# Squares of a head split into rounded parts by halves, and the parts of a head's end at other steps

## The reference

```
proj = h @ w_in;  q, f, i, g = split(proj, 4)
log_f = logaddexp(log(lb), log1p(-lb) + log_sigmoid(f));  k = (1 - lb) * sigmoid(-f)
q = silu(q) * 128 ** -0.5
S_t = diag(f_t) S_{t-1} + k_t v_t^T ;  o_t = S_t^T q_t          # by chunks, per head
o = o * rsqrt(mean(o * o, axis=-1) + 1e-6)                      # per token and head
o = o * out_norm * silu(g);  return o @ w_out
```

## Time and profile before

| | |
|---|---|
| median of 3 runs | 2599.49 us (2598.84 to 2599.61) |
| the profiled execution | 2597.69 us |
| its span, first to last instruction | 2595.9 us |
| TensorE (PE) busy | 2567.7 us, 99% |
| VectorE (DVE) busy | 1739.3 us, 67% |
| ScalarE (ACT) busy | 1172.8 us, 45% |
| GpSimd (POOL) busy | 206.0 us, 8% |
| mean granted TensorE clock | 0.999 |

### The profile page before, as it was taken

How to read it: one execution, slowest core, us unless ns; L and a number is a source line. 1 busy time by engine, 2 the same in 40 slices (tenths; PEclk the granted TensorE clock), 3 DMA queues, 4 the chain that set the end, 5 groups by cost and what they waited for, 6 DMA issues and landing times.

```text
span 2595.9 us, 41811 instructions
## 1 busy us (share of the span) xinstructions
PE 2567.7 (99%) x16880; PEld 2148.2 (83%) x16880; DVE 1739.3 (67%) x2471; ACT 1172.8 (45%) x1844; POOL 206.0 (8%) x245
## 2 busy tenths in 40 slices
PE   8999999999999999999999999999999999999999
PEld 7887878787888887887989878977887888888887
DVE  6454454559999978898725564566667777768573
ACT  6454444536444443356432343244545555554331
POOL 2121222300100001132000000000000000000000
PEclk9999999999999999999999999999999999999999
DMA  4101111235777799983423212121543444487763
GB/s 142 42 26 42 35 41 34 73 124 176 253 242 252 266 375 335 336 294 138 159 87 131 67 60 69 42 76 59 197 157 117 154 154 141 158 326 279 242 223 136
DMA packets 290769, 406.14 MB, mean 156 GB/s; under 512 B 15760, under 2 KB 162704, under 8 KB 290576
## 3 DMA queue, kind: packets, MB, share of 16 engines
q1 hardware_dynamic: 276464, 352.07, 39.7%
q0 software_dynamic: 14112, 51.39, 5.8%
HBM read 314.27 MB, written 89.13 MB: 155 GB/s over the span
## 4 chain that ended last, share of the span: by engine, by line
PE 70%; DVE 6%; DMA 3%; issue 2%; ACT 1%; SPq 0%; DVEq 0%; ACTq 0%
PE ps L973 14%; PE ps L903 7%; PE ps L905 7%; PE ps L901 7%; PE ps L579 3%; PE ps L563 3%; PE ps L566 3%; PE ps L689 3%; PE ps L1160 3%; PE ps L693 3%; PE ps L691 3%; PE ps L1161 2%; PE ps L1165 2%; PE ps L1135 1%; DVE mraw L2460 1%
## 5 line engine op out<-in xcount | busy, mean ns | idle before, releaser
L901 PE MATMUL ps<-Bh,Ah 128*128 128x512 f32 x896 | 349.6, 390 | 1.4 <-ACT vb L1715 1.4
L903 PE MATMUL ps<-Bh,Al 128*128 128x512 f32 x896 | 348.8, 389 | 1.5 <-DVE Al L2336 1.5
L2127 DVE TENSOR_TENSOR Wlo<-Wraw,Whi 128x1024 fp32r<-128x1024 f32 x100 | 124.6, 1262 | 217.5 <-ACT Whi L1533 217.4
L905 PE MATMUL ps<-Bl,Ah 128*128 128x512 f32 x640 | 249.0, 389 | 0.0
L1737 ACT ACTIVATE ftr_h<-ftr_r 128x1024 fp32r<-128x1024 f32 x112 | 118.6, 1059 | 237.6 <-DMA ftr_r<-b_scratch 237.4
L973 PE MATMUL ps<-ftr_l,wgt_h 128*128 128x512 f32 x848 | 210.1, 390 | 4.0 <-DVE ftr_l L2404 4.0
L689 PE MATMUL ps<-Whi,Hh 128*128 128x256 f32 x736 | 212.2, 288 | 0.0
L973 PE MATMUL ps<-ftr_h,wgt_h 128*128 128x512 f32 x848 | 210.0, 390 | 0.0
L973 PE MATMUL ps<-ftr_h,wgt_l 128*128 128x512 f32 x848 | 209.6, 389 | 0.0
L693 PE MATMUL ps<-Whi,Hl 128*128 128x256 f32 x736 | 208.2, 283 | 0.0
L691 PE MATMUL ps<-Wlo,Hh 128*128 128x256 f32 x736 | 208.2, 283 | 0.0
(11 more groups left out here) (383 smaller groups left out, 5463.6 us busy)
## 6 DMA issues: line engine op xcount, KB each, us to landing
b_scratch<-qb SPq DMA_DIRECT2D x224, 256.0 KB, 3.0
wgt_r<-in_m_w SPq DMA_DIRECT2D x112, 512.0 KB, 4.8
ftr_r<-b_scratch SPq DMA_DIRECT2D x112, 512.0 KB, 6.1
pair<-in_m_w SPq DMA_DIRECT2D x128, 256.0 KB, 3.2
mraw<-in_w_ada POOLq DMA_DIRECT2D x64, 512.0 KB, 4.6
Wraw<-in_w_in SPq DMA_DIRECT2D x56, 512.0 KB, 4.1
other<-in_m_w SPq DMA_DIRECT2D x32, 512.0 KB, 5.6
mraw<-in_m_w1T POOLq DMA_DIRECT2D x32, 512.0 KB, 5.1
```

The source lines that it names most:

```text
L901: e.matmul(o, h[:, k, :], Bh[x][:, k, :], start=first and k == 0, stop=False, skip_group_check=not first)
L903: e.matmul(o, l[:, k, :], Bh[x][:, k, :], start=False, stop=False, skip_group_check=not first)
L905: i = e.matmul(o, h[:, k, :], Bl[x][:, k, :], start=False, stop=k == 3, skip_group_check=not first)
L2127: e.tensor_tensor(Wlo[n % 4][:], Wraw[n % 2][:], Whi[n % 4][:].bitcast(F), ALU.subtract).then_inc(*S("w_lo", "v").tick(n))
```

## The change

The squares of a head's outputs are no longer one float32 tile `t1`. ACT squares each half (512 tokens), copies it rounded into `sq_h` (at the place of `t2`), and DVE subtracts that from the square into `sq_l` (at the place of `t1`). Part 3 then sums `sq_h` and `sq_l` of each half with a rounded matrix of ones, `onesR`, in four matmuls of 512 columns. The copy of the outputs to `R1` moves behind the squares on ACT. `onesR` is made once, ahead of the first norm's root. The entries of `tail_steps` become part 0, part 1, nothing, part 2, nothing, nothing, part 3, nothing for heads 0 to 6; head 7 keeps its order.

```diff
--- before.py
+++ after.py
@@ -155,6 +155,8 @@
         near = at("near", [P, 8, 32], F, spare)
         acc, kST, St = sa("acc", 10), sa("kST", 11), sa("St", 12)
         t1, t2, t3 = sa("t1", 13), sa("t2", 14), sa("t3", 15)
+
+        sq_l, sq_h, onesR = sa("sq_l", 13, R), sa("sq_h", 14, R), at("onesR", [P, P], R, spare + 1024)


         H_ = lambda i: HA + 4096 * i
@@ -286,7 +288,8 @@
             return iter([("idle", h, 0)] + [("level", h, l) for l in range(8)])

         def tail_steps(h):
-            return [(("tail", h, i // 2) if i % 2 == 0 else ("idle", h, 0)) for i in range(8)]
+            order = (0, 1, None, 2, None, None, 3, None) if h < 7 else (0, None, 1, None, 2, None, 3, None)
+            return [("idle", h, 0) if p is None else ("tail", h, p) for p in order]

         MIX = [("f_end", 0, None)]
         tail = []
@@ -788,9 +791,11 @@
                             pe.wait_ge(S("q_mul").at((h, 7)), S("q_copy").at((h, 7)), out_at(("tail", h, 1)))
                             i = e.matmul(ps[:, c, :], c3(St)[:, c, :], c3(Qb[h % 2])[:, c, :], start=False, stop=True)
                 else:
-                    pe.wait_ge(out_at(("tail", h, 2), 1))
                     for p, c in enumerate(HALF):
-                        e.matmul(psum[b][:, c], ones[:], t1[:, c], start=True, stop=True).then_inc(
+                        pe.wait_ge(S("const_hi").at(0), S("o_rstd").at((h, p - 2)))
+                        e.matmul(psum[b][:, c], onesR[:], sq_h[:, c], start=True, stop=False)
+                        pe.wait_ge(S("o_gate").at((h, p - 2)))
+                        e.matmul(psum[b][:, c], onesR[:], sq_l[:, c], start=False, stop=True).then_inc(
                             *S("ps_full", b).tick((occ, p)))
                     return
                 full(i, b, occ)
@@ -1580,6 +1585,8 @@
                     feed(2)
                 square(1, k, R1[:, k, :], lambda p: S("x", k).at(0), [(t1 if k == 0 else (t2, t3)[(k - 1) % 2], 1.0)])
             feed(4)
+            act.wait_ge(S("const").at(0))
+            e.activation(onesR[:], ones[:], ACT.Copy).then_inc(*S("const_hi").tick(0))
             rstd("norm1", 1, rstd1)


@@ -1661,11 +1668,14 @@
                             act.wait_ge(full_at(("tail", h - 1, 1)))
                         e.activation(kST[:, 0:896], ps[:, 0:896], ACT.Copy).then_inc(*freed(("tail", h, 0)))
                     elif i == 2:
+                        if h:
+                            act.wait_ge(full_at(("tail", h - 1, 3), 1), S("o").at((h - 1, 1)))
+                        for p, c in enumerate(HALF):
+                            e.activation(t1[:, c], ps[:, c], ACT.Square).then_inc(*freed(("tail", h, 2), p))
+                            act.wait_ge(out_at(("tail", h, 2), p))
+                            e.activation(sq_h[:, c], t1[:, c], ACT.Copy).then_inc(*S("o_rstd").tick((h, p - 2)))
                         act.wait_ge(H1.lo_at(h))
-                        e.activation(R1[:, h, :], ps[:], ACT.Copy).then_inc(*freed(("tail", h, 2), 0))
-                        if h:
-                            act.wait_ge(full_at(("tail", h - 1, 3), 1))
-                        e.activation(t1[:], ps[:], ACT.Square).then_inc(*freed(("tail", h, 2), 1))
+                        e.activation(R1[:, h, :], ps[:], ACT.Copy).then_inc(*freed(("tail", h, 2), 2))
                     elif i == 3:
                         table(LOG)
                         for p, c in enumerate(HALF):
@@ -2263,11 +2273,16 @@
                         x = e.scalar_tensor_tensor(s3[:, c + 1, :], s3[:, c, :], tot[:, c:c + 1], ps[:, c, :], ALU.mult,
                                                    ALU.add)
                         x.then_inc(*(S("state").tick((h, c)) if c < 6 else freed(("tail", h, 1))))
+                elif kind == "tail" and i == 2:
+                    for p, c in enumerate(HALF):
+                        dve.wait_ge(S("o_rstd").at((h, p - 2)), out_at(("tail", h, 2), p))
+                        e.tensor_tensor(sq_l[:, c], t1[:, c], sq_h[:, c].bitcast(F), ALU.subtract).then_inc(
+                            *S("o_gate").tick((h, p - 2)))
                 elif kind == "tail" and i == 3:
                     for p, c in enumerate(HALF):
                         dve.wait_ge(S("o_rstd").at((h, p)), S("g0").at(h))
                         e.tensor_tensor(t2[:, c], t2[:, c], sg[:, c], ALU.mult).then_inc(*S("o_gate").tick((h, p)))
-                        dve.wait_ge(S("o_gate").at((h, p)), out_at(("tail", h, 2), 0))
+                        dve.wait_ge(S("o_gate").at((h, p)), out_at(("tail", h, 2), 2))
                         e.scalar_tensor_tensor(R1[:, h, c], R1[:, h, c], vec[:, V_ON + h:V_ON + h + 1], t2[:, c], ALU.mult,
                                                ALU.mult).then_inc(*S("o").tick((h, p)))
                 elif kind == "split" and h % 2 == 0:
```

## The result

The changed kernel took a median of 2609.65 us in six runs (2604.47 to 2613.2); the kernel before, in as many runs, 2600.12 us (2598.84 to 2601.23). The ratio is 1.0034, with a 95% interval of 1.0023 to 1.0044: slower by 0.34%. The profiled execution of the changed kernel is its fastest run, 2604.47 us with a span of 2602.6. Its two runs with a mean granted clock of 0.999 took 2604.47 and 2604.89 us; the four with 0.995 to 0.998 took 2609.45 to 2613.2.

A forecast was written before the change was run, and what follows sets the result against it. TensorE, busy 99% of the span, was taken to bound the kernel. Tails before odd heads +3.8, tails 1, 3, 5 +2.0, tail 6 +1.3, tail 7 -0.8 made +6.3 us: median 2605.8, range 2602 to 2610.

The forecast's parts named there:

- A: Likeliest rival: the forecast as summed, with a range of 2604 to 2607.5 us; chance 50%.
- B: Rival: longer TensorE waits also lower the clock, 1.7 us a fall, one to three falls giving 2607.5 to 2611; chance 25%.
- Part 1: Sums of squares on TensorE: four rounded matmuls replace two float32 ones, 0.92 us for 1.72, saving 0.80 us per head.
- Part 2: ScalarE and VectorE make the halves: sums with their wait 1.1 us for 2.24, saving 1.15 us in heads 0 to 5.
- T: End of a head's output matmuls on TensorE, from which the start times of the squares, copies and subtractions were counted.
- Part 3: Products with V come earlier but wait 2.27 us for the transposed k's copy: 1.83 us added in heads 0 to 6.
- Part 4: ScalarE's log table load, queued behind the R1 copy, comes 1.27 us later; all of it reaches TensorE before odd heads.
- The page weighed: Skill page's 1380 ns drain per table switch, weighed against the trace: by it the sum would be 10.4 us, not 6.3.
- rival F: A table load right behind a running activation waits for its drain: up to 3.8 us more, 2609.6 us; chance 3%.
- The sum: All head tails together: 3.8 + 2.0 + 1.3 - 0.8 = +6.3 us, median 2605.8 us.
- C: Rival: odd heads lose only what TensorE loses, 4.6 us or less, giving 2601 to 2604.7 us; chance 15%.
- D: Rival: the transposed k's copy is ready early, so its wait vanishes; 8.5 us saved, 2591 us; chance 5%.

The follow-up runs named there:

- kST first on ScalarE: Changed kernel with the copy of the transposed k moved ahead of ScalarE's two sigmoids in heads 0 to 6; 2590.36 us, ratio 0.9956 to the kernel before.
- the three moves: Changed kernel with the transposed k's copy earlier on ScalarE in all eight heads and VectorE's q scaling ahead of the gate multiplies; 2587.10 us, ratio 0.9953.
- The filled wait: Changed kernel with seven idle identity products on TensorE ahead of the products with V in heads 0 to 6; 2604.39 us, ratio 1.0014 to the kernel before.

## Why the prediction was right and where it was off

The range (2602 to 2610) and the sign held, the range with only 0.35 us to spare, and two of the six runs lie above it. 2605.8 was 3.8 us low. The rival held likeliest, A, had a range of its own (2604 to 2607.5), and the median is not in it: what came is A's sum plus B's falls. That the stated range still holds it is in part luck. By its own steps:

- **Part 1, the form of the sums: right.** 4 x 0.23 us in place of 4 x 0.43.
- **Part 2, the parts: right, on the safe side.** The half Square took 0.60 and 0.58 us where I took 0.65, the half copy 0.63, the subtraction 0.69. The last part was ready at T+3.4 (T is 103.07 here), not T+3.5, so t3 waited for nothing where I had 0.15 us.
- **Part 3, the wait for kST: right.** 2.27 us in head 0 as worked out, and kST first on ScalarE removed it. Between the tails the changed kernel loses 1.2 to 1.3 us on the way to and through odd heads (forecast 1.27) and about 0.6 in even ones (0.68).
- **Part 4, the queue behind t3: right in place, a little large.** The load comes 0.81 us later on the clock of the trace, 1.13 with the 0.32 us that this tail starts earlier; I had 1.27. Level 0 of heads 1, 3 and 5 waits 0.6 to 0.7 us more. What I did not see is that VectorE's order, the scaling of q behind four other instructions, decides there; the three moves showed it.
- **The page weighed: the rows decide.** The load starts 0.02 us behind the end of the R1 copy, and Ln starts 0.02 us behind the end of the load. The Trainium skill (ScalarE: Activation LUTs, What ACT_TABLE_LOAD costs) names a drain of about 1380 ns for a switch of set; there is none here, and the 1.28 us that rival F would cost is not there.
- **The sum: right for the mixer.** Forecast 6.3 us, traces 6.2 and 6.4 without the falls. Tail 6 took 1.5 where I had 1.3 (0.86 less 0.46 is 0.4 us sooner, not the 0.5 that I took off); tail 7 gave 0.8 as forecast.
- **The term that was mis-sized is rival B.** I gave the falls of the clock one chance in four and left them out of the likeliest case. They came in both traces of the changed kernel, one and two in the mixer, 1.6 to 3.2 us. The filled wait puts them at 5.3 us of the median. The 1.6 us of a fall that the traces show is what B had priced (1.7). How much of the 5.3 lies outside the mixer stays open: the filled kernel's median is 4.2 over before where its mixer is 6.8 over, so the places outside differ by some 2 us between kernels. The step that failed is "Against: the longest wait of the mixer (1.7 us) left the clock at 1.00". The new waits are 2.2 to 2.5 us, nearer to the stretch in which the clock had fallen (2.24 of 4 us busy) than to the one in which it had not, and there are seven of them in a run. With one to three falls B had said 2607.5 to 2611, and that is where the median lies.
- **C** (2601 to 2604.7) did not come about, and **D**'s condition was made in the experiment with kST first: its 2591 was nearly met by 2590.36, but in part by luck: D took 8.5 us off and the runs show 9.8. It left out the 0.44 us that PE had waited for kST in each of heads 0 to 6 (3.1 us) and the 1.9 us that PE now waits at level 0 of the odd heads; 8.5 + 3.1 - 1.9 is 9.7.

## What to carry to other kernels

A step that one engine runs earlier brings nothing if its operand comes from another engine's queue: before moving it, look at what stands ahead of the operand's producer in that engine's order, and move the producer with it. The same move cost 9.5 us without the producer's and gained 9.8 with it. And a stall on TensorE can cost more than its length: where several waits of over 2 us come in a run, look at the granted clock of the stretch behind each, in more than one execution.

## What the runs showed of the hardware that I had not expected

- Waits of 2.3 us in an otherwise full stream were enough for the granted clock to fall to 1.2 GHz: PE busy for 1.07 of 3 us, then 0.57 over the next 4, at a price of 1.6 us. They do not always bring it down: in the three traces with the new order, kST unmoved and the waits empty, a fall came behind 5 of 21 such waits, and in the changed kernel with kST first the clock stayed up behind a wait of 2.6 us in the first MLP. The heads where it falls change from execution to execution (head 3 in one trace, heads 0 and 5 in another).
- Filling such waits with useless matmuls, at a nearly unchanged stall, lowered the median by 5.3 us.
- The kernel before itself ranges over 9 us (2595.2 to 2604.1) in 23 runs, where its first three had agreed within 0.8.
